# Moving the attention's value products by one step, behind the next pair's first transposes

## What is computed

```python
def _attend(q, k, v, sink):
    s = jnp.einsum('bqkgd,bnkd->bkgqn', q, k, preferred_element_type=jnp.float32)
    ...
        p = jax.nn.softmax(s, axis=-1)
    return jnp.einsum('bkgqn,bnkd->bqkgd', p.astype(v.dtype), v)

def _merge(h, outs, gates, w_br, w_merge, b_merge, w_out):
    yb = jnp.stack([o * jax.nn.silu(z) for o, z in zip(outs, gates)], axis=2)
    y = jnp.einsum('bnrw,rwd->bnrd', yb, w_br)
    g = jax.nn.sigmoid(h @ w_merge + b_merge).reshape(b, n, N_BRANCH, D_MODEL)
    return jnp.sum(g * y, axis=2) @ w_out
```

## Time and profile before

| | |
|---|---|
| median of 3 runs | 2836.05 us (2835.54 to 2838.32) |
| profiled execution, own time | 2840.35 us |
| its span, first to last instruction | 2838.5 us |
| granted TensorE clock, mean over the span | 0.991 |
| TensorE busy | 2763.2 us (97%) |
| VectorE busy | 1354.7 us (48%) |
| ScalarE busy | 845.9 us (30%) |
| GpSimd busy | 1362.5 us (48%) |

### The profile page before, as it was taken

How to read it: one execution, slowest core, us unless ns; L and a number is a source line. 1 busy time by engine, 2 the same in 40 slices (tenths; PEclk the granted TensorE clock), 3 DMA queues, 4 the chain that set the end, 5 groups by cost and what they waited for, 6 DMA issues and landing times.

```text
span 2838.5 us, 36730 instructions
## 1 busy us (share of the span) xinstructions
PE 2763.2 (97%) x14580; PEld 2166.7 (76%) x14580; DVE 1354.7 (48%) x2233; ACT 845.9 (30%) x1582; POOL 1362.5 (48%) x1114
## 2 busy tenths in 40 slices
PE   7999999999999999999999999999999999999998
PEld 5988777777888877677897666788787755788886
DVE  4421556676546123435946765524725946511113
ACT  3011432331130143322325354232233235222222
POOL 2445223224535644558766545844545423744443
PEclk9999999999999999999999999999999989999998
DMA  7112222222321221223321212232323311332322
GB/s 272 49 47 66 67 79 86 71 92 82 128 78 60 90 63 56 75 89 116 96 75 61 74 45 82 86 103 82 96 92 106 119 43 63 101 95 86 100 87 76
DMA packets 241718, 243.76 MB, mean 86 GB/s; under 512 B 5344, under 2 KB 228448, under 8 KB 240928
## 3 DMA queue, kind: packets, MB, share of 16 engines
q1 hardware_dynamic: 240256, 237.89, 26.2%
q0 software_dynamic: 1312, 3.80, 0.5%
HBM read 233.16 MB, written 7.34 MB: 85 GB/s over the span
## 4 chain that ended last, share of the span: by engine, by line
PE 86%; DVE 9%; ACT 2%; issue 1%; POOL 1%; DMA 0%; SPq 0%; DVEq 0%; POOLq 0%; ACTq 0%
PE psum L959 23%; PE psum L961 22%; PE psum L960 22%; PE psum L1230 4%; PE psum L1209 1%; DVE columns L2720 1%; PE psum L1166 1%; PE psum L1185 1%; POOL columns L3438 1%; PE psum L1508 1%; PE psum L1165 1%; PE psum L1234 1%; PE psum L1349 1%; PE psum L1528 1%; DVE columns L2538 1%
## 5 line engine op out<-in xcount | busy, mean ns | idle before, releaser
L959 PE MATMUL psum<-columns,columns 128*128 128x512 f32 (+1 forms) x3464 | 1337.0, 386 | 12.4 <-DVE columns L2530 3.1
L961 PE MATMUL psum<-columns,columns 128*128 128x512 f32 (+1 forms) x3464 | 1262.4, 364 | 0.0
L960 PE MATMUL psum<-columns,columns 128*128 128x512 f32 (+1 forms) x3464 | 1260.8, 364 | 0.0
L3438 POOL TENSOR_TENSOR columns<-columns,columns 128x512 fp32r<-128x512 f32 (+1 forms) x676 | 904.1, 1367 | 436.3 <-ACT columns L1904 403.8
L3434 POOL TENSOR_TENSOR columns<-columns,columns 128x512 fp32r<-128x512 f32 x392 | 423.6, 1111 | 924.5 <-PE psum L961 750.5
L959 PEld LDWEIGHTS psum<-columns,columns 128*128 128x128 f32 x3464 | 654.0, 189 | 185.6 <-issue 68.1
L960 PEld LDWEIGHTS psum<-columns,columns 128*128 128x128 f32 x3464 | 654.4, 189 | 121.1 <-issue 24.2
L961 PEld LDWEIGHTS psum<-columns,columns 128*128 128x128 f32 x3464 | 653.0, 189 | 111.6
L1904 ACT ACTIVATE columns<-columns 128x1024 fp32r<-128x1024 f32 (+2 forms) x154 | 136.7, 936 | 172.4 <-PE psum L961 166.1
L2720 DVE SCALAR_TENSOR_TENSOR columns<-columns,columns,columns 128x256 f32<-128x256 f32 x224 | 154.1, 743 | 0.0
L2702 DVE SCALAR_TENSOR_TENSOR columns<-columns,psum 128x512 f32<-128x512 f32 x80 | 54.8, 685 | 186.1 <-PE psum L1230 181.2
(11 more groups left out here) (433 smaller groups left out, 2679.6 us busy)
## 6 DMA issues: line engine op xcount, KB each, us to landing
columns<-in_w_merge SPq DMA_DIRECT2D x32, 1024.0 KB, 6.6
columns<-in_w_in SPq DMA_DIRECT2D x22, 1024.0 KB, 5.4
columns<-in_ev_w_in SPq DMA_DIRECT2D x22, 1024.0 KB, 5.2
columns<-in_ffn_gate SPq DMA_DIRECT2D x22, 1024.0 KB, 5.3
columns<-in_ffn_up SPq DMA_DIRECT2D x22, 1024.0 KB, 5.3
columns<-in_w_ada SPq DMA_DIRECT2D x18, 1024.0 KB, 5.5
columns<-in_ffn_down SPq DMA_DIRECT2D x16, 768.0 KB, 4.7
columns<-in_ffn_down SPq DMA_DIRECT2D x16, 640.0 KB, 4.2
```

What stands on the lines that cost most here:

```text
L959: mm(dst, weights(0, k), moving(0, k), start=start and k == 0, stop=False)
L960: mm(dst, weights(0, k), moving(1, k), start=False, stop=False)
L961: last = mm(dst, weights(1, k), moving(0, k), start=False, stop=stop and k == k_tiles - 1)
L3438: last = g.tensor_tensor(low[:, c], raw[:, c], high[:, c].bitcast(F32), ALU.subtract)
```

## The change

The products with the values go from phase 13 of the pair's second unit to phase 14. With units six steps apart, phase 14 of unit u is phase 8 of unit u + 1: the step of the next pair's first transposes. These stand earlier in the code, so within the step the transposes come first and the products behind them. Nothing else is touched; the waits ahead of the products stay the same ones.

```diff
@@ -1192,7 +1192,7 @@
                         last = nc.tensor.transpose(psum[:, t_at + (j - 4) * P:t_at + (j - 3) * P], prob[:, u % 2, j * P:(j + 1) * P], ident)
                     last.then_inc(rest_turned, 1)
 
-                u = unit_at(l, step, 13)
+                u = unit_at(l, step, 14)
                 if u is not None and u % 2 == 1:
                     b, t, _ = units[u]
                     pe.wait_ge(first_copied, base + u + 1)
```

## The result

| | before | changed |
|---|---|---|
| median, 8 runs each | 2837.06 us (2835.54 to 2842.05) | 2843.91 us (2840.44 to 2846.23) |
| ratio, 95% interval | | 1.0019 (1.0011 to 1.0028) |
| span of the profiled execution | 2838.5 us | 2844.4 us |

The ratio comes to 5.4 us, with an interval of 3.1 to 7.9 us; the two medians by themselves lie 6.9 us apart.

The account below looks back on a forecast made before the run. TensorE, busy for 97% of the span, was taken to bound the kernel. Junctions -0.2, lost cover +4.1 and waiters 0 summed to +3.9 us, from a median of 2836.05 to 2840.0 us; range 2835.3 to 2844.8.

Parts of the forecast that it names:

- (a) the junctions: TensorE's entries into and exits from the products among new neighbours: transposes to products 0.20 us, 0.2 us gained in all.
- (b) the cover: Time the products gave the scaled probabilities before layer 0's next first transposes; seven places fall short, 4.1 us lost.
- The recoveries: Units 28 and 32, layer 0: 1.23 and 1.2 us lost at first transposes, regained at rest transposes; loss 0.
- (c): Those waiting for the products, ScalarE's copy and VectorE's gate: later input stays covered, cost 0.
- The sum: All terms for the whole kernel: -0.2 + 4.1 + 0 = +3.9 us, 0.14% slower on the median.
- the free junction: Rival: transposes to products takes only 0.11 us, so +0.4 us in all, 2836.5 us; chance 0.12.
- the failed recoveries: Rival: at units 28 and 32 the copy comes later too and TensorE waits again; +6.3 us, 2842.4 us; chance 0.13.
- The junction dearer than read: Rival: transposes to products from 0.25 us up passes 0.2%; at 0.33 it is +8.7 us, 2844.8 us; chance 0.07.
- No cover is lost: Rival: VectorE and ScalarE come earlier too, so first transposes don't wait; -0.2 us, 2835.9 us; chance 0.10.
- the copy or gate is hurt by the later step: Rival named with the experiments: the later step itself costs, +4 us or more even with products ahead of transposes; no chance given.

Follow-up runs that it names:

- five pairs moved alone: Against the kernel before, only the products ahead of layer 0's units 20, 24, 36, 40 and 44 go one step later; 1.0016 (1.0007 to 1.0025).
- The other runs of the same loss: Against the kernel before, products one step later in layer 0 alone, 1.0017, or only ahead of its units 20, 24, 36, 40 and 44, 1.0016.
- the 31 moved pairs: Against the kernel before, products one step later except ahead of layer 0's units 20, 24, 28, 32, 36, 40, 44; 0.9997 (0.9988 to 1.0006).
- the one with products first: Against the kernel before, products at the later step as in the change, but ahead of that step's transposes in the code; 0.9993 (0.9984 to 1.0002).
- the kernel before with the taper: Kernel before with VectorE's modulation products six steps later, in the last three rounds only 4, 2 and 0; 0.9991 (0.9982 to 1.0000).

## Why the prediction was right

- **(a) the junctions**: transposes to products was taken as 0.20 us from another attention's rows, and is 0.20 at all 38 places. In layer 1, which has only this part of the change, it cost 0.13 us where 0.0 was said; the kernels without the change in layer 1 differ by up to 0.06 us there. The prediction counted 28 + 12 places for the 38 that move (26 + 12), which changes nothing. The products' first weight load starts with its matmul in the changed kernel too (1 to 2 ns ahead in all 40 groups), behind an idle of 0.17 us on the load side. The rule of the Trainium skill (TensorE: Matmul & The Clock Gate, Step-by-step: what each phase is for), that weight loads are pulled ahead of matmuls in flight where the row groups don't conflict or the background buffer is the target, isn't borne out for this first load. Inside the group it is: in all 40 groups the third load starts 0.11 us before its matmul.

```profile
504.66 0.85 PEld L1209 LDWEIGHTS psum<-columns,columns 128*64 128x64 f32 x16 [0.17 <-issue]
504.67 1.10 PE L1209 MATMUL psum<-columns,columns 128*64 128x128 f32 x16
```

- **(b) the cover**: seven places in layer 0, none in layer 1, units 4, 8 and 12 just in time (0.17 to 0.18 us to spare). The loss of each place is read from the distance of the transposes' start from the matmul ahead of them, against the same distance in the kernel before, with 0.06 us added for the longer group where it did not wait before: unit 20 gave 0.8 us (0.71 said), 24 0.8 (0.79), 36 1.0 (1.02), 40 0.7 (0.76), 44 0.7 (0.79). Together 4.0 us where 4.1 was said, and five pairs moved alone made 3.95 us.
- **The recoveries** at units 28 and 32 held: the products fill the wait in front of the rest transposes. The waits at the first transposes grew by 5.8 us (5 to 7 said), those at the rest shrank by 2.5 us (2.5 said).
- **(c)** the last gate's wait was 1.9 us as before, and the products wait for nothing.
- **The sum** was +3.9 us. The two stretches together grew by 4.2 us; the time by 5.4 us (3.1 to 7.9). The interval holds both. The other runs of the same loss gave 4.8 and 4.5 us, so a second cost of 1 us or more is not shown, and not ruled out either. The median of 2843.91 us lies 3.9 us above the forecast one: 1.0 us because the kernel before has 2837.06 us over eight runs and not 2836.05, the rest because the medians are 6.9 us apart and not 3.9. That it still fell inside the range is in part luck.
- Of the rivals, the free junction and the failed recoveries are out by the rows above. The junction dearer than read is out by the 0.20 us at 38 places and by the 31 moved pairs that cost less than 0.2 us. "No cover is lost" is out by the pair of experiments on five pairs and on the 31. That the copy or gate is hurt by the later step is out by the one with products first, for the modulation products at their old place; with these moved, the last gate leaves it open, as said above.

## What to carry to other kernels

A group of instructions that waits for nothing can still be worth its place: what stands directly behind it may need its time as cover. Before moving it, take its length off the start of everything it used to precede and hold that against the end of each input, place by place; a mean or a single pair would have shown nothing here, since 31 of 38 pairs had room. The same list says where the loss comes back: a group put in front of a later wait of the same chain fills that wait.

## What had not been expected

- VectorE's modulation products (`L2720`) got faster by being moved. Groups of instructions in layer 0's stretch (count, then busy us and mean ns), before and then the kernel before with the taper:

```profile
L2720 DVE SCALAR_TENSOR_TENSOR columns<-columns,columns,columns 128x256 f32<-128x256 f32 x166 | 110.1, 715 | 0.0
```

```profile
L2720 DVE SCALAR_TENSOR_TENSOR columns<-columns,columns,columns 128x256 f32<-128x256 f32 x168 | 76.7, 510 | 0.0
```

The same instruction takes 715 ns in the mean where it runs in the first 16 of 24 steps and 510 ns six steps later. The two traces show where this comes from: GpSimd's splitting. Of the 166 before, the 120 beside which no GpSimd instruction ran took 460 to 484 ns, and the 46 beside one took 704 to 1535 ns, 1337 in the mean. With the taper only 10 of 168 ran beside one, and the other 158 took 465 to 485 ns.
- Entering the 64-column products costs some 0.1 us over the usual distance to the next matmul, behind 128 columns (0.20 us and not 0.11) as behind 512 (0.33 and not 0.23), and leaving them costs another 0.1 us (the second matmul behind them starts 0.34 us after the first and not 0.23). None of the moves tried saves that, except next to a group that hides a part of it: with the transposes behind, a pair gained 0.05 us.
